# One 512-column product in place of two 256-column ones in the xbc slots, with VectorE summing the two halves

## The chip, the cores and the metric

The kernel runs on one core of one Trainium2 chip. The metric is the device time of one execution in microseconds. Three executions of the kernel before took 1444.45, 1445.17 and 1445.17 us, median 1445.17.

## The reference, cut to what matters

Two transformer blocks are computed for 256 tokens of width 1024 in fp32. The change touches the second block's mixer, and there one piece:

```
h   = rmsnorm_2(x, norm_mix_w)
u   = h @ w_in                                   # 1024 -> 3760 columns
z, xbc, dt = split(u_ssd)                        # xbc: 2048 columns
xbc = silu(causal_depthwise_conv(xbc, conv_w, conv_b))   # 4 taps along the tokens
xs, bm, cm = split(xbc)                          # feed the chunked state-space scan
```

The rest of the mixer is a 16-head latent attention (called mla here) on other columns of `u`, then the output projection.

## The kernel before, in words

Every weight matrix comes in slots of 128 x 1024 fp32. SyncE loads slot n into `ring` (three deep). ScalarE rounds it into `w_hi` (the cast, L1563), GpSimd subtracts to get the low part `w_lo` in two halves of 512 columns (L521), and TensorE multiplies. A product of fp32 quality is three products of rounded operands: high weight by high x, high weight by low x, low weight by high x. GpSimd's two halves of a slot read `ring` and `w_hi`, both in SBUF. In the expert stage VectorE does this subtraction and GpSimd does none.

The normed x stands in `h_both`, [128, 8 blocks, 512]: columns 0 to 255 of a block hold its high part, 256 to 511 its low part. The tuple `h_t` names the two halves.

The 2048 xbc columns are 16 slots, walked in the order `XBC`, each position `pos` with a PSUM bank `XBC_BANK[pos]` (2, 3, 0, 1, and then 0 and 1 in turn). `channels_slot` does one slot on TensorE: once the slot is rounded, for each of 8 blocks k the high weight block times both halves of x (L563 and L564, 256 columns each, into the same 256 columns of the bank); once the low part is there, 8 more products (L568); then it raises `spent`. A slot at `pos` of 4 or more first waits until the convolution of position `pos - 2` is done (`conv_done >= 4 * (pos - 1)`), because that one used the same bank.

On VectorE `conv(pos)` waits for `spent`, multiplies the bank's 256 columns by the row of 1/rms factors `row_x` (L2894, in place in PSUM), and applies four taps: one `tensor_scalar` (L2896) and three `scalar_tensor_tensor` (L2900), each waiting for the one before it by semaphore. ScalarE applies silu later, four positions at a time.

The order is written out by hand on each engine. On TensorE: positions 0 to 3; then 17 units of the two up-projections of the attention (`up`, L572, L573, L577), whose results VectorE and ScalarE copy out of alternate bank pairs (`up_copied`, L2912 and L2915 on VectorE; a third chunk of units may start only when the first is copied); then position 4, turns, position 5, scores of heads 0 and 1, position 6; and then the head loop, h = 0 to 15: `mla_scores(h + 2)`, `mla_turn(h)`, other turns, and `xbc(7 + h)` for h up to 8. After position 15 (h = 8) the heads 9 to 12 carry the late slots of z (`z_late`), whose second half of the first slot waits for `xdt_made >= 2`.

On VectorE: convolutions 0, 1, 2, first copy, convolution 3, more copies and rotations, convolution 4, mask and maximum of heads 0 and 1, convolution 5, and then per head h: `inverse(h + 1)`, `masked(h + 2)` (L2972, L2975), the copy of the turned probabilities (L3031), `conv(6 + h)` for h up to 9, and at some heads one of `out_lo` (L3001), `cb_mask` (L2986, L2987) or `xs_out` (L2995, L2996; the second of them raises `xdt_made` to 2 at head 8). ScalarE runs the exponentials between the masks and the inverses. Each engine takes its own list strictly in order.

Another stage holds the two forms that the change uses. The ffn's up-projection multiplies `w_hi` by a whole 512-column block of `h_both` (L1500) and the low part by 256 columns (L1503). The expert stage sums the halves of a bank with `tensor_reduce` over `"p (m t) -> p t m"` (L2792).

Of the kernel before, what the change touches and what calls it, by code (L numbers as in the profile page):

```python
# [22 lines left out]
ALU = mybir.AluOpType  # L23
# [5 lines left out]
AX = mybir.AxisListType.X  # L29

P = 128
T, D = 256, 1024
TT = T // P
KD = D // P
# [16 lines left out]
NS = 3  # L51
# [88 lines left out]
XBC_STEP = [STEP["xbc_first"] + i for i in range(4)] + [STEP["xbc"] + i for i in range(12)]  # L140
XBC_BANK = [2, 3, 0, 1] + [0, 1] * 6
# [151 lines left out]
def two_blocks(nc, weights, consts, cols_in, rows_in, x_in, mem_in, pos_in, out):  # L293
    with ExitStack() as ctx:
# [12 lines left out]
        h_both = sb("h_both", [P, KD, 2 * T], F32R)  # L307
        h_t = h_both[:, :, 0:T], h_both[:, :, T:2 * T]
        cst = sb("cst", [P, NCONST])
        cols = sb("cols", [P, NCOLS])  # L310
        rows = sb("rows", [P, NROWS])
# [13 lines left out]
        bank = ctx.enter_context(nc.psum_tensor("bank", [P, 8, 512], F32))  # L325

        def area(name, pattern=None, **kw):
            a, b = AREA[name]
            v = arena[:, a:b]
            return v.rearrange(pattern, **kw) if pattern else v  # L330
# [123 lines left out]
        def wait_slot(pe, n):  # L454

            pe.wait_ge(s["split"], n + 1)

        def wait_rounded(pe, n):

            pe.wait_ge(s["hi_made"], n + 1)  # L460
# [90 lines left out]
        def _(pe):  # L551
# [27 lines left out]
            def channels_slot(n, out_, src, ready=None):  # L579

                wait_rounded(pe, n)
                for k in range(KD):
                    if ready:
                        ready(k)
                    rounded_w(out_, both(w_parts, every, n % NS, slice(k * P, (k + 1) * P)), both(src, every, k, slice(0, T)),
                              start=(k == 0))
                wait_slot(pe, n)
                for k in range(KD):
                    mm = rest_w(out_, both(w_parts, every, n % NS, slice(k * P, (k + 1) * P)), both(src, every, k, slice(0, T)),
                                stop=(k == KD - 1))  # L590
                mm.then_inc(s["spent"], 1)
# [53 lines left out]
            every = slice(0, P)  # L645
            w_parts = (w_hi, w_lo)
# [117 lines left out]
            for i in range(5):  # L764
                g = row("diff_g") if i == 0 else row("ret_g")[:, (i - 1) * P:i * P]
                mm = pe.matmul(bank[:, 5, i:i + 1], g, ident[:, 0:1], start=True, stop=True)
# [163 lines left out]
            for i, (what, b, at) in enumerate(QUERY_ORDER):  # L930
                n = QUERY_SLOT[i]
# [210 lines left out]
            def xbc(pos):  # L1142

                if pos == 2:
                    pe.wait_ge(s["copied_act"], z0 + 2)
                if pos >= 4:
                    pe.wait_ge(s["conv_done"], 4 * (pos - 1))
                channels_slot(XBC_STEP[pos], bank[:, XBC_BANK[pos], 0:T], h_t)

            for pos in range(4):  # L1150
                xbc(pos)
# [1108 lines left out]
        def _(dve):  # L2260
# [626 lines left out]
            row_copied(area("row_x"), bank[:, 7, 0:T], 1)  # L2887
            by_head = lambda a: a.rearrange("p (h c) -> p h c", c=64)

            def conv(pos):  # L2890
                j = XBC[pos]
                dve.wait_ge(s["spent"], XBC_STEP[pos] + 1)
                b = bank[:, XBC_BANK[pos], :]
                v.tensor_tensor(b[:, 0:T], b[:, 0:T], area("row_x"), ALU.mult).then_inc(s["xbc_scaled"], 1)  # L2894
                dve.wait_ge(s["xbc_scaled"], pos + 1)
                v.tensor_scalar(xc[:, j, :], b[:, 0:T], col("xw", 4 * j + 3), col("xb", j), ALU.mult, ALU.add)\  # L2896
                    .then_inc(s["conv_done"], 1)
                for d in range(1, 4):
                    dve.wait_ge(s["conv_done"], 4 * pos + d)
                    v.scalar_tensor_tensor(out=xc[:, j, d:T], in0=b[:, 0:T - d], scalar=col("xw", 4 * j + 3 - d),  # L2900
                                           in1=xc[:, j, d:T], op0=ALU.mult, op1=ALU.add).then_inc(s["conv_done"], 1)
# [422 lines left out]
```

## Time and profile before

| | |
|---|---|
| runs of the kernel before | 1444.45, 1445.17, 1445.17 us |
| the profiled execution | 1444.22 us, its span 1442.4 us |
| TensorE matmuls, busy share of the span | 99%, 8796 instructions |
| VectorE | 66%, 2036 instructions |
| ScalarE | 58%, 1509 instructions |
| GpSimd | 62%, 717 instructions |
| granted TensorE clock | 0.998 of full speed |

Times in a profile row are microseconds from the start of the span unless they are called ns. PE is the matmul engine TensorE and PEld its loading of the stationary operand, DVE is VectorE, ACT ScalarE, POOL GpSimd. A matmul's own duration includes its way through the array, so matmuls in a stream overlap: the pace is read from the starts, or from the pieces of the chain. `[idle <- releaser]` behind an instruction is how long its engine sat before it and what ended that.

### The profile page before, as it was taken

What the parts mean: (1) busy time and instruction counts of PE and PEld (TensorE: products, weight loads), DVE (VectorE), ACT (ScalarE), POOL (GpSimd) and SP (SyncE); (2) the same over time, 40 slices, a digit from 0 to 9 for tenths busy, and PEclk for the clock granted to TensorE, in tenths of its full rate; (3) what the DMA queues carried; (4) which work ended last, traced back from release to release, by engine and by line L of the source; (5) the groups of instructions that cost most, each with busy time, mean ns of one, the idle gap of its engine ahead of it and who ended that gap; (6) DMA issues with size and microseconds to landing.
All of it is one profiled execution on the core that took longest, in us unless ns stands there. A gap on an engine that the chain in (4) does not pass through costs nothing.

```text
span 1442.4 us, 25571 instructions
## 1 busy us (share of the span) xinstructions
PE 1428.8 (99%) x8796; PEld 1275.7 (88%) x8796; DVE 946.3 (66%) x2036; ACT 835.1 (58%) x1509; POOL 899.0 (62%) x717
## 2 busy tenths in 40 slices
PE   8999999999999999999999999999999999999997
PEld 6788999999999999888888888888898889888886
DVE  4564399978889998655555554335677733477776
ACT  6576555456666666455445444448687765544454
POOL 6749898987777778100000006998954576699996
PEclk9999999999999999999999999999999999999999
DMA  7535567655555555555555555665633454465554
GB/s 257 161 103 180 180 196 235 195 171 161 157 165 162 162 156 163 185 200 195 197 190 191 197 195 186 192 184 185 196 129 103 164 158 138 137 193 189 191 188 131
DMA packets 137589, 253.08 MB, mean 175 GB/s; under 512 B 16464, under 2 KB 18896, under 8 KB 136848
## 3 DMA queue, kind: packets, MB, share of 16 engines
q1 hardware_dynamic: 135392, 243.79, 52.8%
q10 hardware_dynamic: 1872, 6.41, 1.3%
q0 software_dynamic: 224, 1.54, 0.3%
q8 instruction: 62, 1.02, 0.3%
q14 instruction: 39, 0.32, 0.1%
HBM read 248.54 MB, written 3.15 MB: 174 GB/s over the span
## 4 chain that ended last, share of the span: by engine, by line
PE 96%; POOL 1%; DVE 1%; issue 1%; ACT 1%; DMA 0%; SPq 0%; POOLq 0%; DVEq 0%; ACTq 0%
PE bank L554 13%; PE bank L555 13%; PE bank L556 13%; PE bank L577 6%; PE bank L572 6%; PE bank L573 6%; PE bank L568 5%; PE bank L1500 5%; PE bank L563 5%; PE bank L564 5%; PE bank L1503 3%; PE bank L1028 2%; PE bank L1001 2%; PE bank L1031 1%; POOL w_both L521 1%; PE bank L1240 1%
## 5 line engine op out<-in xcount | busy, mean ns | idle before, releaser
L521 POOL TENSOR_TENSOR w_both<-ring,w_both 128x512 fp32r<-128x512 f32 x694 | 881.5, 1300 | 527.7 <-ACT w_both L1563 519.4
L1563 ACT CAST w_both<-ring 128x1024 fp32r<-128x1024 f32 x452 | 474.3, 1050 | 368.4 <-PE bank L556 176.3
L2766 DVE TENSOR_TENSOR w_both<-ring,w_both 128x1024 fp32r<-128x1024 f32 x108 | 132.3, 1225 | 121.1 <-ACT w_both L1563 119.8
L554 PE MATMUL bank<-w_both,act_hi 128*128 128x512 f32 x512 | 199.8, 390 | 0.4 <-DVE act_lo L2771 0.4
L555 PE MATMUL bank<-w_both,act_hi 128*128 128x512 f32 x512 | 199.6, 390 | 0.0
L556 PE MATMUL bank<-w_both,act_lo 128*128 128x512 f32 x512 | 199.4, 389 | 0.0
L555 PE MATMUL bank<-h_both,w_both 128*128 128x256 f32 x648 | 183.6, 283 | 0.0
L554 PE MATMUL bank<-h_both,w_both 128*128 128x256 f32 x648 | 183.6, 283 | 0.0
L556 PE MATMUL bank<-h_both,w_both 128*128 128x256 f32 x648 | 183.6, 283 | 0.0
L563 PE MATMUL bank<-h_both,w_both 128*128 128x256 f32 x544 | 135.7, 288 | 0.0
L564 PE MATMUL bank<-h_both,w_both 128*128 128x256 f32 x544 | 133.3, 283 | 0.0
L554 PEld LDWEIGHTS bank<-h_both,w_both 128*128 128x128 f32 x648 | 124.5, 192 | 0.0
L556 PEld LDWEIGHTS bank<-h_both,w_both 128*128 128x128 f32 x648 | 124.5, 192 | 0.0
L555 PEld LDWEIGHTS bank<-h_both,w_both 128*128 128x128 f32 x648 | 124.5, 192 | 0.0
L554 PEld LDWEIGHTS bank<-w_both,act_hi 128*128 128x128 f32 x512 | 96.2, 188 | 20.6 <-DVE w_both L2766 0.7
L556 PEld LDWEIGHTS bank<-w_both,act_lo 128*128 128x128 f32 x512 | 96.2, 188 | 19.9
L555 PEld LDWEIGHTS bank<-w_both,act_hi 128*128 128x128 f32 x512 | 96.3, 188 | 19.1
L564 PEld LDWEIGHTS bank<-h_both,w_both 128*128 128x128 f32 x544 | 104.4, 192 | 0.2
L563 PEld LDWEIGHTS bank<-h_both,w_both 128*128 128x128 f32 x544 | 104.2, 192 | 0.4 <-DVE arena L2900 0.2
L2718 DVE TENSOR_TENSOR hots<-bank,chosen_t 128x1024 fp32r<-128x1024 f32 x64 | 78.3, 1224 | 11.1 <-PE bank L1001 7.1
L572 PE MATMUL bank<-w_both,h_both 128*128 128x512 f32 (+2 forms) x208 | 81.8, 395 | 0.3 <-issue 0.3
L568 PE MATMUL bank<-h_both,w_both 128*128 128x256 f32 x576 | 80.5, 283 | 0.0
(479 smaller groups left out, 2719.8 us busy)
## 6 DMA issues: line engine op xcount, KB each, us to landing
ring<-weights_in SPq DMA_DIRECT2D x910, 256.0 KB, 3.0
mem_kv<-arena ACTq DMA_DIRECT2D x2, 1024.0 KB, 7.1
arena<-mem_kv ACTq DMA_DIRECT2D x2, 1024.0 KB, 7.7
ring<-weights_in SPq DMA_DIRECT2D x8, 200.0 KB, 2.6
ring<-weights_in SPq DMA_DIRECT2D x8, 144.0 KB, 2.7
xres<-x_in SPq DMA_DIRECT2D x2, 512.0 KB, 5.1
arena<-mem_in POOLq DMA_DIRECT2D x1, 1024.0 KB, 8.5
arena<-rows_in ACTq DMA_DIRECT2D x2, 512.0 KB, 4.3
```

Source lines behind the costliest of these rows:

```text
L521: nc.gpsimd.tensor_tensor(w_lo[:, k, at], ring[:, k, at], w_hi[:, k, at].bitcast(F32), ALU.subtract).then_inc(s[done], 1)
L554: pe.matmul(out_, a[0], b[0], start=start, stop=False, **kw)
L555: pe.matmul(out_, a[0], b[1], start=False, stop=False, **kw)
L556: return pe.matmul(out_, a[1], b[0], start=False, stop=stop, **kw)
L563: pe.matmul(out_, w[0], b[0], start=start, stop=False, skip_group_check=True)
L564: return pe.matmul(out_, w[0], b[1], start=False, stop=False, skip_group_check=True)
L568: return pe.matmul(out_, w[1], b[0], start=False, stop=stop, skip_group_check=True)
L572: pe.matmul(out_, x[0], w[0], start=start, stop=False, skip_group_check=True)
L573: return pe.matmul(out_, x[1], w[0], start=False, stop=False, skip_group_check=True)
L577: return pe.matmul(out_, x[0], w[1], start=False, stop=stop, skip_group_check=True)
L1563: nc.scalar.copy(w_hi[:, k, :], ring[:, k, :]).then_inc(s["hi_made"], 1)
L2766: v.tensor_tensor(w_lo[:, k, :], ring[:, k, :], w_hi[:, k, :].bitcast(F32), ALU.subtract)\
```

## The change

In `xbc(pos)` the call of `channels_slot` is replaced. The high weight block now multiplies the whole 512-column block of `h_both` in one instruction, so that the bank's columns 0 to 255 collect high weight by high x and columns 256 to 511 high weight by low x; the low weight products go into columns 0 to 255 as before. `conv(pos)` first sums the bank's two halves into `xbc_sum`, 256 columns of `rows` in SBUF, and the multiplication by `row_x` takes `xbc_sum` in place of the bank. A wait on `xbc_scaled` stands between the two. The waits on `conv_done`, the banks and the order of the work stay.

```diff
-                channels_slot(XBC_STEP[pos], bank[:, XBC_BANK[pos], 0:T], h_t)
+                n, to = XBC_STEP[pos], bank[:, XBC_BANK[pos], :]
+                w = lambda k: both(w_parts, every, n % NS, slice(k * P, (k + 1) * P))
+                wait_rounded(pe, n)
+                for k in range(KD):
+                    pe.matmul(to, w(k)[0], h_both[:, k, :], start=(k == 0), stop=False, skip_group_check=True)
+                wait_slot(pe, n)
+                for k in range(KD):
+                    mm = rest_w(to[:, 0:T], w(k), both(h_t, every, k, slice(0, T)), stop=(k == KD - 1))
+                mm.then_inc(s["spent"], 1)
...
+            xbc_sum = rows[:, 0:T]
+
             def conv(pos):
                 j = XBC[pos]
                 dve.wait_ge(s["spent"], XBC_STEP[pos] + 1)
                 b = bank[:, XBC_BANK[pos], :]
-                v.tensor_tensor(b[:, 0:T], b[:, 0:T], area("row_x"), ALU.mult).then_inc(s["xbc_scaled"], 1)
-                dve.wait_ge(s["xbc_scaled"], pos + 1)
+                v.tensor_reduce(xbc_sum, b.rearrange("p (m t) -> p t m", m=2), AX, ALU.add).then_inc(s["xbc_scaled"], 1)
+                dve.wait_ge(s["xbc_scaled"], 2 * pos + 1)
+                v.tensor_tensor(b[:, 0:T], xbc_sum, area("row_x"), ALU.mult).then_inc(s["xbc_scaled"], 1)
+                dve.wait_ge(s["xbc_scaled"], 2 * pos + 2)
```

## Rows read from the trace of the kernel before

**Rows 1.** The page: busy us (share of the span), and the chain by engine.
```profile
PE 1428.8 (99%) x8796; PEld 1275.7 (88%) x8796; DVE 946.3 (66%) x2036; ACT 835.1 (58%) x1509; POOL 899.0 (62%) x717
...
PE 96%; POOL 1%; DVE 1%; issue 1%; ACT 1%; DMA 0%; SPq 0%; POOLq 0%; DVEq 0%; ACTq 0%
```

**Rows 2.** Busy us and instructions of each engine by stretch.
```profile
core 0: us, PE busy (x) PEld busy (x) DVE busy (x) ACT busy (x) POOL busy (x), PEclk, DMA share, GB/s
1008.70:1020.25 11.55, 11.55 (x98) 11.55 (x97) 7.50 (x16) 8.23 (x12) 10.80 (x10) 1.00 0.66 196
...
1056.40:1106.80 50.40, 50.40 (x394) 46.48 (x393) 43.07 (x113) 38.13 (x91) 23.69 (x19) 1.00 0.30 95
```

**Rows 3.** Loads of the stationary operand in order of time, two that waited for VectorE.
```profile
1056.40 0.19 PEld L563 LDWEIGHTS bank<-h_both,w_both 128*128 128x128 f32 x1 [0.16 <-DVE arena L2900]
...
1106.84 0.19 PEld L572 LDWEIGHTS bank<-w_both,h_both 128*128 128x128 f32 x1 [0.28 <-DVE arena L2996]
```

**Rows 4.** Pieces of the chain: start, us on the chain, what.
```profile
1008.74 0.12 PE bank L563
...
1010.64 0.96 PE bank L568 x8
...
1280.10 1.81 PE bank L1500 x8
1281.91 0.95 PE bank L1503 x8
```

**Rows 5.** VectorE's groups by line: count, busy us, mean ns.
```profile
L2792 DVE TENSOR_REDUCE work<-bank 128x256 f32<-128x512 f32 x19 | 13.1, 691 | 47.5 <-PE bank L1031 47.5
...
L2771 DVE TENSOR_TENSOR act_lo<-arena,act_hi 128x256 fp32r<-128x256 f32 x108 | 47.5, 441 | 0.5 <-ACT act_hi L1869 0.5
```

**Rows 6.** VectorE in order of time: convolution 0 and the next start.
```profile
1016.41 0.43 DVE L2894 TENSOR_TENSOR bank<-bank,arena 128x256 f32<-128x256 f32 x1
1016.88 0.54 DVE L2896 TENSOR_SCALAR arena<-bank,cols 128x256 f32<-128x256 f32 x1
1017.46 1.52 DVE L2900 SCALAR_TENSOR_TENSOR arena<-bank,cols,arena 128x255 f32<-128x255 f32 x3
1018.90 0.42 DVE L2894 TENSOR_TENSOR bank<-bank,arena 128x256 f32<-128x256 f32 x1
```

**Rows 7.** VectorE and GpSimd in order of time, at two VectorE instructions.
```profile
1043.63 1.31 POOL L521 TENSOR_TENSOR w_both<-ring,w_both 128x512 fp32r<-128x512 f32 x1
1044.22 1.00 DVE L2958 TENSOR_TENSOR arena<-arena 128x256 f32<-128x256 f32 x1
1044.88 1.50 POOL L521 TENSOR_TENSOR w_both<-ring,w_both 128x512 fp32r<-128x512 f32 x1
...
1060.75 1.27 POOL L521 TENSOR_TENSOR w_both<-ring,w_both 128x512 fp32r<-128x512 f32 x1 [1.83 <-ACT w_both L1563]
1061.32 0.74 DVE L3041 TENSOR_TENSOR head_one<-cst 128x16 fp32r<-128x16 f32 x1
```

**Rows 8.** All waits of VectorE, 1056.4 to 1106.8: us, times, longest.
```profile
DVE bank L2972 <- PE bank L1240: 1.8, 3, 1.0
DVE arena L2986 <- PE bank L1213: 1.5, 2, 0.9
DVE arena L2981 <- ACT work L2018: 1.4, 2, 1.0
DVE arena L3039 <- PE bank L1202: 0.8, 1, 0.8
```

**Rows 9.** GpSimd in order of time: three of its slots in the head loop.
```profile
1052.10 2.54 POOL L521 TENSOR_TENSOR w_both<-ring,w_both 128x512 fp32r<-128x512 f32 x2 [1.99 <-ACT w_both L1563]
...
1074.70 2.55 POOL L521 TENSOR_TENSOR w_both<-ring,w_both 128x512 fp32r<-128x512 f32 x2 [5.61 <-ACT w_both L1563]
...
1097.78 2.53 POOL L521 TENSOR_TENSOR w_both<-ring,w_both 128x512 fp32r<-128x512 f32 x2 [6.05 <-ACT w_both L1563]
```

**Rows 10.** VectorE in order of time: the first copy of the up-projections, and head 0's mask.
```profile
1024.39 0.75 DVE L2912 TENSOR_SCALAR arena<-bank,arena 128x512 f32<-128x512 f32 x1 [0.47 <-PE bank L577]
...
1051.65 0.43 DVE L2972 TENSOR_TENSOR bank<-bank,arena 128x256 f32<-128x256 f32 x1 [2.78 <-PE bank L1240]
```

## The prediction, made before the changed kernel was run

> **What bounds the kernel now.** I read the page first. TensorE is busy for 99% of the span and makes 96% of the chain that ended last [rows 1]. So time saved on TensorE comes out at the end, unless another engine is then late. The busy times by stretch come next [rows 2]. In the head loop, 1056.4 to 1106.8, where positions 7 to 15 run, TensorE is full, but VectorE is busy for 43.07 of 50.40 us, 85%, far above its 66% over the span. GpSimd is busy for 23.69 us, 47%; in the stretch of the first four positions it is busy for 10.80 of 11.55 us. Last, the waits of the weight loads [rows 3]: only twice around the change does TensorE wait for VectorE. At 1056.40 (position 7) it waits 0.16 us for the last tap of convolution 5. At 1106.84 (second half of the first z_late slot) it waits 0.28 us for L2996, the `xs_out` behind convolution 14. At these two places VectorE is already the late one, so work added to it ahead of them goes into the time.
>
> **TensorE's part.** Before, a slot has 16 high-weight products, a piece of 0.12 each on the chain, and 8 low ones in 0.96 us, so 0.12 each and 16 x 0.12 = 1.92 us for the high part [rows 4]. After, the high part is 8 products of 512 columns. The ffn has the same instruction with the same operands: 8 in 1.81 us [rows 4]. The gain is 1.92 - 1.81 = 0.10 us a slot (between 0.08 and 0.11, as the 1.81 and 0.96 are read), 16 x 0.10 = 1.6 us in all. The low part stays.
>
> The Trainium skill ("TensorE: Matmul & The Clock Gate", section "Back-to-back issue gap") puts an isolated warm gap at N/2.4 + 2.5 ns, so a merge would save 2.5 ns, 0.3 us in all. The rows of this case disagree: 0.12 us for 256 columns and 1.81/8 = 0.226 for 512 leave 0.014 us for each instruction saved. I go by the rows.
>
> **VectorE's part, the sum.** Each convolution gets one more `tensor_reduce` from PSUM, 512 elements to 256 with the same access pattern as L2792: 691 ns [rows 5]. It adds a wait by semaphore between two dependent instructions. Today L2894 lasts 0.43 us and the next starts 0.47 us after it [rows 6], so 0.04 of handing over. The step costs 0.69 + 0.04 = 0.73 us, for 16 convolutions 11.7 us of VectorE.
>
> **VectorE's part, the multiplication.** It now reads two operands from SBUF, `xbc_sum` and `row_x`; before, one came from PSUM. Its own length stays about 0.42 us (L2771, two SBUF operands, same size, takes 441 ns where GpSimd is idle [rows 5]). But rows 7 show what such an instruction does beside GpSimd. L2958 has two SBUF operands and 256 elements; it starts at 1044.22, while GpSimd's half slot runs from 1043.63 to 1044.94, and it lasts 1.00 us, to 1045.22: it stood until GpSimd was through. GpSimd's next half took 1.50 us in place of 1.27. L3041 with 16 elements lasts 0.74 us, to 1062.06, where GpSimd's half ends at 1062.02. L2894, with an operand in PSUM, starts at 1016.41 inside such a stretch of GpSimd and takes 0.43. So each multiplication that meets a half slot of GpSimd waits for its end, between 0 and 1.27 us, and in half the cases 0.2 us are put on GpSimd.
>
> The Trainium skill states this as a rule ("SBUF — State Buffer", section "Who interferes with whom"): a VectorE instruction with two SBUF inputs contends with a GpSimd instruction that reads SBUF, and whoever starts first holds the shared read port for its whole length. By that rule the trace agrees, with the 1.00 us above; `tensor_reduce` is named there as free of it.
>
> **What lies beside other work.** Convolutions 0 to 2 stand ahead of the first copy, which today starts at 1024.39 with 0.47 us of idle time before it [rows 10]. They add 3 x 0.73 = 2.2 us and their waits, three times at most 1.27. GpSimd is nearly full here, so a mean of 0.6 each: the copy starts 2.2 + 1.8 - 0.5 = 3.5 us later and ends, 0.75 long, at 1028.6. Three units of six 512-column products, 18 x 0.227 = 4.1 us, lie between the end of the first chunk at about 1024.3 and the chunk that needs the copy, at 1028.4, or 1028.0 with 0.4 us gained by then. So I count at most a stall of 0.6 here, none if the waits are short; up to 2.5 if all are long. I take 0. The same cover serves convolution 3, and VectorE then waits for TensorE again. Convolution 4 ends well before the scores of head 0, for which VectorE waits 2.78 us today [rows 10]. So at the scores of head 0 TensorE and VectorE both stand 0.6 us earlier (six slots).
>
> **What lies on the path.** From there to the `xs_out` that TensorE waits for, VectorE's list holds convolutions 5 to 14, ten of them. Ten sums: 10 x 0.73 = 7.3 us. VectorE's idle time on this stretch is 1.8 + 1.5 + 1.4 + 0.8 = 5.5 us [rows 8], and it takes up that much. The waits for the port: I laid the ten multiplications, moved by what had collected, on GpSimd's slots, moved with the TensorE slot that frees them. A slot takes 2.54 us of some 5.6. Three multiplications fall into one: convolution 5 (into the slot of 1052.10), 9 (1074.70) and 13 (1097.78) [rows 9], with 0.6, 0.75 and 0.8 us; the others fall beside. That is 2.2 us. By chance alone it would be 10 x 0.47 x 0.64 = 3.0; the ends are 0 and 10 x 1.27.
>
> The sum: -0.6 + 7.3 + 2.2 - 5.5 = +3.4 us when `xs_out` of head 8 is done. TensorE stands there already, since it gained on every slot; its gains on positions 6 to 15 are spent in waiting. What is late on the way: position 7 for convolution 5 (instead of 0.16 about 1.6 us), then position 11 for convolution 9, and last the z_late slot. Behind the stretched convolution on VectorE stand inverse, mask and copy of the next head; ScalarE's exponentials follow the mask, but each mask runs two heads ahead of the turn that needs it, so I count nothing for them. Convolution 15 comes after; no more convolutions follow it and VectorE comes back to waiting for scores. From there all engines run 3.4 us later, and TensorE fills the chain to the end. Weights are loaded ahead, the 0.2 us put on GpSimd now and then is covered there. SyncE's loads follow GpSimd and stay ahead too.
>
> The profiled execution took 1444.22 us with a span of 1442.4, so 1.8 outside. I forecast a span of 1445.8 and a profiled execution of 1447.6. The median shown is 0.95 above the profiled execution; against it I forecast 1445.17 + 3.4 = 1448.6 us.
>
> **The rivals.**
> - *No waiting for the port.* The multiplication costs what it did, 0.42. Against it speak L2958 and L3041 [rows 7]; for it, that a wait shows only where the two meet, and the phases may fall well. Then -0.6 + 7.3 - 5.5 = +1.2 us: 1446.4.
> - *TensorE keeps its gain*, the other side. VectorE's sums are taken up by its idle time everywhere, and the time falls by 1.6: 1443.6. It is decided at the z_late slot: VectorE may collect no more than its 5.5 us of idle time minus the 1.0 that TensorE gains on positions 6 to 15 before it. Ten sums would have to cost under 0.45 us each. For it: 34% of VectorE's span is idle. Against it: 0.69 for the same form, and the 0.28 us already waited there.
> - *The waits are long*, with GpSimd in step with VectorE, as both follow TensorE's slots, and the first copy is late too: ten times 0.9 and 1 to 2 us in the up-projections make -0.6 + 7.3 + 9 - 5.5 + 1.5 = +11.7 at most; with half of that waiting +6 to +7, 1452.
> - *The merge brings less* than in the ffn. Then the first six slots give 0 in place of 0.6, and the time is +4.0: a part of the forecast's own range.
>
> **How the numbers follow.** 0.2% of this kernel's time is 2.9 us, and what lies within it can hardly be told from no change. The forecast, +2.2 to +5, has 0.50, of it about 0.35 above 2.9. No waiting for the port has 0.24, within the bound. TensorE keeps its gain: 0.10, a third of which may come out below -2.9 or be some gain I don't see. Long waits: 0.15, all slower; 0.01 for the rest. So slower 0.50, same 0.46, faster 0.04. The range from 1445.7 to 1453.0 holds the forecast, the first rival and most of the long waits; the forecast's own range is 1447.4 to 1450.2.
>
> **What would show it.** In the profile after: 128 TensorE instructions fewer; the group of 512-column products in the xbc slots at 0.227 apart; a `tensor_reduce` x16 of 0.69 us; the multiplication x16 with a mean well above 0.42 and single ones near 1 us or more, each ending just behind a half slot of GpSimd. The weight load of position 7 should wait 1 to 2 us for a tap, and the z_late load 2 to 4 us for L2996's successor. VectorE's idle time in the head loop should fall below 2 us. I am wrong if the multiplications all stay at 0.42, if the z_late load does not wait longer, or if the span changes by more than that one stage does.

## The result, and the profile after

The changed kernel took 1449.62 us (median of 7 runs, 1448.18 to 1451.18), the kernel before in the same session 1445.13 (7 runs, 1444.12 to 1445.17). The ratio is 1.0033, 95% interval 1.0023 to 1.0043: slower by 4.5 us, where 3.4 were forecast. The profiled execution took 1450.12 us, its span 1448.3.

I compare the traces by three legs of the stage, each between two starts: from the first high-weight load of the xbc slots to the scores of head 0 (up-projections); from there to the second instruction of the second `xs_out`, which releases the late z slot (head loop); from there to the last `seg` product on VectorE, some 49 us on (last leg).

| us | first load | scores 0 | `xs_out` | last `seg` | legs | sum |
|---|---|---|---|---|---|---|
| before | 1008.47 | 1050.60 | 1106.10 | 1154.83 | 42.13, 55.50, 48.73 | 146.36 |
| after | 1009.16 | 1051.88 | 1110.41 | 1160.66 | 42.72, 58.53, 50.25 | 151.50 |

So +0.6 in the up-projections, +3.0 in the head loop, +1.5 in the last leg, 5.1 together. Another 0.7 of the 5.9 us between the spans lies ahead of the first load, where the code is the same; the first load starts between 1007.6 and 1009.4 in the profiles of all twelve kernels, so that is scatter.

The page of the changed kernel, its busy times and its chain by engine:

```profile
PE 1431.5 (99%) x8668; PEld 1269.4 (88%) x8668; DVE 960.5 (66%) x2052; ACT 835.7 (58%) x1509; POOL 900.3 (62%) x717
...
PE 92%; DVE 4%; POOL 1%; issue 1%; ACT 1%; DMA 0%; SPq 0%; POOLq 0%; DVEq 0%; ACTq 0%
```

Against [rows 1] TensorE has 128 instructions fewer and VectorE 16 more; VectorE's share of the chain went from 1% to 4%. The chain of the changed kernel at its first slots (start, us, what) shows TensorE's part as it was forecast:

```profile
1009.43 1.85 PE bank L1152 x8
1011.29 0.95 PE bank L568 x8
1012.24 1.84 PE bank L1152 x8
```

A slot now takes 1.85 + 0.95 = 2.80 us; before, from one group of low products to the next it was 2.88, so the gain is 0.08 a slot.

The head-loop leg by stretch, of the changed kernel and then of the one before (columns as in [rows 2]):

```profile
1051.88:1110.41 58.53, 56.18 (x359) 47.70 (x357) 54.61 (x133) 43.44 (x105) 27.92 (x22) 1.00 0.32 99
```

```profile
1050.60:1106.10 55.50, 55.50 (x436) 51.55 (x435) 46.91 (x122) 42.88 (x105) 25.55 (x21) 1.00 0.32 100
```

VectorE is busy for 54.61 - 46.91 = 7.70 us more and idle for 3.92 in place of 8.59 us, 4.67 less: 7.70 - 4.67 = 3.03, the whole difference of the leg. TensorE, full before, stands for 2.35 us of the leg. Where it stands is in its weight loads in order of time, changed kernel:

```profile
1058.40 1.68 PEld L1152 LDWEIGHTS bank<-h_both,w_both 128*128 128x128 f32 x8 [0.97 <-DVE arena L2912]
...
1081.55 1.69 PEld L1152 LDWEIGHTS bank<-h_both,w_both 128*128 128x128 f32 x8 [0.58 <-DVE arena L2912]
...
1111.14 0.19 PEld L572 LDWEIGHTS bank<-w_both,h_both 128*128 128x128 f32 x1 [2.48 <-DVE arena L3008]
```

Positions 7 and 11 wait for convolutions 5 and 9, and the late z slot waits 2.48 us where it waited 0.28 [rows 3]. VectorE's two instructions of the change, as groups of the stretch 1010 to 1120 of the changed kernel:

```profile
L2906 DVE TENSOR_TENSOR bank<-rows,arena 128x256 f32<-128x256 f32 x16 | 11.0, 690 | 0.6
L2904 DVE TENSOR_REDUCE rows<-bank 128x256 f32<-128x512 f32 x16 | 10.9, 681 | 1.4 <-PE bank L568 1.4
```

The sum is 681 ns, as [rows 5] had it. The multiplication has a mean of 690 against 0.42, and single ones tell why; VectorE first, then GpSimd, both in order of time:

```profile
1055.78 0.43 DVE L2906 TENSOR_TENSOR bank<-rows,arena 128x256 f32<-128x256 f32 x1
...
1078.00 1.37 DVE L2906 TENSOR_TENSOR bank<-rows,arena 128x256 f32<-128x256 f32 x1
...
1100.38 1.13 DVE L2906 TENSOR_TENSOR bank<-rows,arena 128x256 f32<-128x256 f32 x1
```

```profile
1053.37 2.54 POOL L521 TENSOR_TENSOR w_both<-ring,w_both 128x512 fp32r<-128x512 f32 x2 [1.85 <-ACT w_both L1571]
...
1076.55 2.54 POOL L521 TENSOR_TENSOR w_both<-ring,w_both 128x512 fp32r<-128x512 f32 x2 [5.61 <-ACT w_both L1571]
...
1099.92 2.71 POOL L521 TENSOR_TENSOR w_both<-ring,w_both 128x512 fp32r<-128x512 f32 x2 [6.06 <-ACT w_both L1571]
```

Convolutions 9 and 13 start their multiplication while GpSimd is at a slot and take 1.37 and 1.13; convolution 5 meets the last 0.13 us of one and takes 0.43. In the full trace every multiplication that starts inside a GpSimd half, long or short, ends 0.28 to 0.30 us behind the end of that half: convolution 9 at 1079.37, with the half over at 1079.09, and convolution 5 at 1056.21, with the half over at 1055.91.

The chain of the changed kernel ahead of the late z slot is convolution 14 and what stands behind it on VectorE:

```profile
1105.90 0.46 DVE work L3043
1106.36 0.61 DVE rows L2904
1106.99 0.45 DVE bank L2906
...
1109.89 0.60 DVE arena L3007
1110.49 0.61 DVE arena L3008
1111.15 0.50 PE bank L572
```

And then what I had not forecast at all. The stretches behind that stall (the granted clock is the third number from the end), and two TensorE groups in them:

```profile
1112.00:1113.00 1.00, 1.00 (x5) 0.76 (x4) 1.00 (x3) 0.82 (x5) 0.00 (x0) 0.64 0.42 154
1113.00:1114.00 1.00, 1.00 (x5) 0.35 (x5) 0.93 (x3) 0.10 (x2) 0.00 (x0) 0.50 0.09 16
1114.00:1115.00 1.00, 1.00 (x6) 0.62 (x8) 0.93 (x3) 0.92 (x1) 0.00 (x0) 0.50 0.00 0
1115.00:1116.00 1.00, 1.00 (x9) 0.67 (x6) 0.85 (x3) 0.58 (x3) 0.80 (x1) 0.65 0.00 0
```

```profile
1112.18 1.81 PE L577 MATMUL bank<-w_both,h_both 128*128 128x512 f32 x4
1113.92 1.55 PE L1269 MATMUL bank<-work,arena 128*64 128x256 f32 x8
```

TensorE had stood from 1109.1 to 1111.15; then its clock is at 0.50 of full, the level of 1.2 GHz, from between 1112 and 1113 to between 1115 and 1116. By the four rows it is there for (0.36 + 0.50 + 0.50 + 0.35) / 0.5 = 3.4 us. The kernel before has a clock of 1.00 here throughout, and the same two groups in it:

```profile
1107.87 1.08 PE L577 MATMUL bank<-w_both,h_both 128*128 128x512 f32 x4
1108.88 0.87 PE L1261 MATMUL bank<-work,arena 128*64 128x256 f32 x8
```

The differences, 0.73 + 0.68 = 1.41, are nearly all of the last leg's 1.52 us.

The up-projections: the first copy on VectorE and TensorE's load behind it, changed kernel.

```profile
1028.29 0.74 DVE L2924 TENSOR_SCALAR arena<-bank,arena 128x512 f32<-128x512 f32 x1
```

```profile
1029.10 0.19 PEld L572 LDWEIGHTS bank<-w_both,lat_hi 128*128 128x128 f32 x1 [0.72 <-issue]
1033.67 0.19 PEld L572 LDWEIGHTS bank<-w_both,lat_hi 128*128 128x128 f32 x1 [0.59 <-issue]
```

The copy comes at 1028.29, in place of 1024.39 [rows 10], and TensorE's load starts 0.07 us behind its end, 1029.03, after 0.72 us of standing. The trace gives "issue" as the cause; by the times it is the copy.

### The profile page after: what moved, and what is told of

It is laid out like the page before. It is cut to its first block, busy times and chain, and to the rows that moved or that the text cites. A ratio compares the mean times of both kernels' runs of the same rounds, so it can differ in the third digit from the quotient of the medians.

```text
span 1448.3 us, 25331 instructions
## 1 busy us (share of the span) xinstructions
PE 1431.5 (99%) x8668; PEld 1269.4 (88%) x8668; DVE 960.5 (66%) x2052; ACT 835.7 (58%) x1509; POOL 900.3 (62%) x717
## 4 chain that ended last, share of the span: by engine, by line
PE 92%; DVE 4%; POOL 1%; issue 1%; ACT 1%; DMA 0%; SPq 0%; POOLq 0%; DVEq 0%; ACTq 0%
PE bank L554 13%; PE bank L555 13%; PE bank L556 13%; PE bank L577 6%; PE bank L572 6%; PE bank L573 6%; PE bank L1508 5%; PE bank L568 5%; PE bank L563 4%; PE bank L564 4%; PE bank L1511 3%; PE bank L1028 2%; PE bank L1001 2%; PE bank L1031 1%; POOL w_both L521 1%
## 5 line engine op out<-in xcount | busy, mean ns | idle before, releaser
L555 PE MATMUL bank<-h_both,w_both 128*128 128x256 f32 x648 | 183.4, 283 | 0.0
L554 PE MATMUL bank<-h_both,w_both 128*128 128x256 f32 x648 | 183.3, 283 | 0.0
L556 PE MATMUL bank<-h_both,w_both 128*128 128x256 f32 x648 | 183.3, 283 | 0.0
L556 PEld LDWEIGHTS bank<-h_both,w_both 128*128 128x128 f32 x648 | 124.4, 192 | 0.0
L554 PEld LDWEIGHTS bank<-h_both,w_both 128*128 128x128 f32 x648 | 124.3, 192 | 0.0
L555 PEld LDWEIGHTS bank<-h_both,w_both 128*128 128x128 f32 x648 | 124.3, 192 | 0.0
L563 PE MATMUL bank<-h_both,w_both 128*128 128x256 f32 x416 | 103.2, 286 | 0.0
L564 PE MATMUL bank<-h_both,w_both 128*128 128x256 f32 x416 | 102.0, 283 | 0.0
L2726 DVE TENSOR_TENSOR hots<-bank,chosen_t 128x1024 fp32r<-128x1024 f32 x64 | 78.4, 1224 | 11.1 <-PE bank L1001 7.0
L568 PE MATMUL bank<-h_both,w_both 128*128 128x256 f32 x576 | 80.4, 283 | 0.0
L1508 PE MATMUL bank<-h_both,w_both 128*128 128x512 f32 x320 | 79.7, 391 | 0.3 <-issue 0.3
L564 PEld LDWEIGHTS bank<-h_both,w_both 128*128 128x128 f32 x416 | 79.8, 192 | 0.2
```

The source lines that it names most:

```text
L554: pe.matmul(out_, a[0], b[0], start=start, stop=False, **kw)
L555: pe.matmul(out_, a[0], b[1], start=False, stop=False, **kw)
L556: return pe.matmul(out_, a[1], b[0], start=False, stop=stop, **kw)
L563: pe.matmul(out_, w[0], b[0], start=start, stop=False, skip_group_check=True)
L564: return pe.matmul(out_, w[0], b[1], start=False, stop=False, skip_group_check=True)
L568: return pe.matmul(out_, w[1], b[0], start=False, stop=stop, skip_group_check=True)
```

## The experiments

My theory after the result: VectorE's sums and its waits for GpSimd make the head loop later, the stall that they leave at the late z slot costs a second time by the clock, and the first convolutions delay the up-projections a little. The rivals are named with each kernel. In the table "wait" is that of the late z load, the ratio is that of the fast executions (it differs from the quotient of the medians by up to 0.0004), and legs and waits are those of one profiled execution of each kernel; the medians of before are 1444.28 us for the first four (33 runs), 1444.44 for the next four (30) and 1444.59 for the last two (18).

| kernel | median us | ratio, 95% | legs | sum | wait |
|---|---|---|---|---|---|
| before | | | 42.13, 55.50, 48.73 | 146.36 | 0.28 |
| after | 1449.62 | 1.0033, 1.0023 to 1.0043 | 42.72, 58.53, 50.25 | 151.50 | 2.48 |
| e1_sum_unused | 1445.43 | 1.0011, 1.0002 to 1.0020 | 41.85, 57.23, 48.70 | 147.78 | 1.85 |
| e2_products_only | 1443.90 | 0.9996, 0.9986 to 1.0005 | 42.32, 55.05, 48.70 | 146.07 | 0.50 |
| e3_sum_only | 1446.75 | 1.0014, 1.0005 to 1.0023 | 42.13, 57.68, 48.70 | 148.51 | 1.69 |
| e4_port_only | 1445.95 | 1.0012, 1.0003 to 1.0021 | 42.15, 56.81, 48.75 | 147.71 | 0.87 |
| e5_first_five | 1444.85 | 1.0004, 0.9995 to 1.0013 | 41.71, 55.50, 48.75 | 145.96 | 0.28 |
| e6_filled | 1449.30 | 1.0034, 1.0023 to 1.0045 | 43.84, 58.53, 48.73 | 151.10 | 0.64 |
| e7_stall_alone | 1447.83 | 1.0020, 1.0010 to 1.0029 | 42.67, 57.67, 50.26 | 150.60 | 2.45 |
| e8_two_later | 1446.67 | 1.0019, 1.0010 to 1.0028 | 43.52, 55.95, 49.08 | 148.55 | none |
| e9_scalar_copies | 1446.68 | 1.0016, 1.0007 to 1.0025 | 43.31, 57.29, 48.73 | 149.33 | 2.02 |
| e10_last_twelve | 1448.75 | 1.0026, 1.0016 to 1.0037 | 42.25, 58.55, 50.30 | 151.10 | 2.47 |

Against before, median and legs agree within 0.9 us. The first leg scatters most: even e7, whose code there is that of before, has 42.67. The last one is steady (48.70 to 48.75 in eight kernels), and the parts of the loop leg add up below, so I read mechanisms from those two.

### The three parts, each by itself

**e1_sum_unused**: the changed kernel, but the multiplication reads columns 0 to 255 of the bank; nobody reads the sum, and the low part of x is left out.

```diff
-                v.tensor_tensor(b[:, 0:T], xbc_sum, area("row_x"), ALU.mult)...
+                v.tensor_tensor(b[:, 0:T], b[:, 0:T], area("row_x"), ALU.mult)...
```

> The changed kernel, but the multiplication by row_x reads the bank's columns 0 to 255 (PSUM) again; the sum is still made into rows and nobody reads it, so the low part of x is left out of the convolution's input. One SBUF operand in place of two, all else the same. Theory (the multiplication waits for GpSimd's half slot): L2906, whose mean was 690 ns, goes back to 0.42 us with none near 1 us; the first copy of the up-projections comes over 2 us earlier, the load at the z_late slot waits 1 to 1.5 us in place of 2.48, and the clock stays at full speed behind it. Time 0.5 to 1.5 us above the kernel before, 3 to 4 below the changed one. Rival (only the length of the 16 sums matters, the port does not): the multiplications drop but the time stays 4 to 4.5 us above before.

**e2_products_only**: TensorE's part alone; the sum is gone as well, and the low part of x is left out.

```diff
-                v.tensor_reduce(xbc_sum, b.rearrange("p (m t) -> p t m", m=2), AX, ALU.add)...
-                v.tensor_tensor(b[:, 0:T], xbc_sum, area("row_x"), ALU.mult)...
+                v.tensor_tensor(b[:, 0:T], b[:, 0:T], area("row_x"), ALU.mult)...
```

> The changed kernel without the sum: 512-column products on TensorE, VectorE multiplies the bank's columns 0 to 255 as before and leaves the low part of x out. Theory (the merge saves 0.08 to 0.10 us a slot): 1.3 to 1.6 us faster than before, minus nothing, since VectorE's list is the old one; the z_late load waits 1 us longer than the 0.28 of before, which gives back up to 1.0: so between -0.6 and -1.6. Rival (a 512-column product costs what two of 256 cost): within 0.2 us of before.

**e3_sum_only**: the kernel before with a sum of the same form (256 columns read twice) ahead of each convolution.

```diff
+                v.tensor_reduce(rows[:, 0:T], b[:, 0:T].unsqueeze(2).broadcast_to([P, T, 2]), AX, ALU.add)...
+                dve.wait_ge(s["xbc_scaled"], 2 * pos + 1)
```

> The kernel before with one more tensor_reduce of 512 reads to 256 outputs in every convolution (it reads columns 0 to 255 of the bank twice and writes rows, which nobody reads), old 256-column products, old multiplication. Theory (VectorE's list binds at position 7 and at z_late): ten sums of 0.73 less VectorE's 5.5 us of idle time, +1.5 to +2.5 us above before; the z_late load waits about 2 us. Rival (VectorE has 34% of idle time and hides 11.7 us of sums): no change, the z_late load waits 0.3 to 0.5 us.

**e4_port_only**: the kernel before, with the multiplication reading two operands from SBUF; the products are left out of the convolution's input.

```diff
-                v.tensor_tensor(b[:, 0:T], b[:, 0:T], area("row_x"), ALU.mult)...
+                v.tensor_tensor(b[:, 0:T], rows[:, 0:T], area("row_x"), ALU.mult)...
```

> The kernel before with one edit: the multiplication reads columns 0 to 255 of rows (SBUF) in place of the bank, so the convolution's input is left out. No sum, old products. Theory (two SBUF operands wait for GpSimd's half slot): the multiplication's mean rises from 0.42 to 0.6 or 0.7 us, single ones to over 1 us, each ending 0.3 to 0.4 us behind the end of a half slot of GpSimd; the waits are mostly taken up by VectorE's idle time, so the time rises by 0 to +1 us only. Rival (the longer multiplications in the changed kernel come from the wait on the sum just ahead, not from the port): here all 16 stay at 0.42 us.

The head-loop legs fit together to some hundredths of a us. The products alone: 55.05 - 55.50 = -0.45. The sum: 57.23 - 55.05 = +2.18 on top of the products, and 57.68 - 55.50 = +2.18 by itself. The multiplication from SBUF: 58.53 - 57.23 = +1.30 in the changed kernel, 56.81 - 55.50 = +1.31 by itself. Together -0.45 + 2.18 + 1.30 = +3.03. Each of these numbers comes from one profile of a kernel. So of the 3.48 us that VectorE's parts cost in the loop, 2.18 are the sum's and 1.30 the multiplication's. In e1 all sixteen multiplications take 431 to 433 ns; in e4 they spread (0.42 to 1.27 us). Its group, two single ones, and its weight load at the late z slot:

```profile
L2894 DVE TENSOR_TENSOR bank<-rows,arena 128x256 f32<-128x256 f32 x16 | 11.7, 729 | 1.1 <-PE bank L568 1.1
```

```profile
1054.37 1.13 DVE L2894 TENSOR_TENSOR bank<-rows,arena 128x256 f32<-128x256 f32 x1
...
1103.99 1.02 DVE L2894 TENSOR_TENSOR bank<-rows,arena 128x256 f32<-128x256 f32 x1
```

```profile
1108.72 0.19 PEld L572 LDWEIGHTS bank<-w_both,h_both 128*128 128x128 f32 x1 [0.87 <-DVE arena L2996]
```

By the Trainium skill ("SBUF — State Buffer", "Who interferes with whom") a VectorE instruction with two SBUF inputs contends with a GpSimd instruction that reads SBUF, and one with at most one SBUF input, outside the 2-port modes, does not. The pair e1 and e4 agrees, 0.43 always against a mean of 0.73. I had put e4 at 0 to +1 us, on the ground that VectorE's idle time would take it up; it cost 1.3 in the loop and 1.7 in the median. The two rows shown are convolution 5, 0.7 us longer straight ahead of position 7, where TensorE waits 0.87 in place of 0.16, and convolution 14, 0.6 longer straight ahead of the late z slot; behind neither is there idle time before TensorE needs the result.

Of the other expectations here, e3's held (+2.5 us, a wait of 1.69). In e1 the time held (+1.2), but the late z load waits 1.85 and not 1 to 1.5. e2's failed: I had put it at -0.6 to -1.6 us, and it came out at -0.4 in the median and -0.3 in the legs. Its slots do start 2.79 us apart, so its rival, that a 512-column product costs what two of 256 do, is out as well; but the gain of the first six slots does not show in its up-projection leg (42.32 against 42.13), which has single waits of 0.52 and 0.42 us where before has none above 0.05.

In none of these four does the clock fall, and in none is the last leg above 48.75. e1 stands close below the changed kernel at the late z slot:

```profile
1107.44 0.19 PEld L572 LDWEIGHTS bank<-w_both,h_both 128*128 128x128 f32 x1 [1.85 <-DVE arena L3008]
```

With 0.6 us less standing than the changed kernel it lost nothing behind it. Of the changed kernel's loss of 5.1 us, 3.0 are in the loop, 0.6 in the up-projections, and the 1.5 of the last leg are in none of its parts.

### The clock

**e7_stall_alone**: the kernel before with three sums, each waiting for the one before it, ahead of the second `xs_out`. Nobody reads them.

```diff
+                if i == 1:
+                    for r in range(3):
+                        link(v.tensor_reduce(rows[:, r * T:(r + 1) * T], bank[:, at, :].rearrange("p (m t) -> p t m", m=2), AX, ALU.add))
```

> The kernel before with one artificial delay: three tensor_reduces of 0.69 us on dead columns of rows, one after the other, ahead of the xs_out for which the z_late slot waits (2.2 us). Nothing else changed. Theory: TensorE waits 0.28 + 2.2 = 2.5 us there, and the granted clock falls behind it as in the changed kernel: +2.2 for the stall and up to +1.5 for the clock, +2.2 to +3.7. If the clock does not fall, +2.2. Rival (later stages take the delay up): under +1.

**e6_filled**: the changed kernel, TensorE repeating the products of the first half of the late z slot ahead of the wait.

```diff
-                    for k in (2 * i, 2 * i + 1):
-                        rounded_x(bank[:, 7 - 4 * t, :], x(k, t), w(k), start=(k == 0))
+                    for _ in range(3 if i == 0 and t == 0 else 1):
+                        for k in (2 * i, 2 * i + 1):
+                            rounded_x(bank[:, 7 - 4 * t, :], x(k, t), w(k), start=(k == 0))
```

> The changed kernel with TensorE busy in the stall at the z_late slot: the first half's eight products are done three times over (each round starts the sum anew, the output is the same), 1.8 us of work in place of waiting; 0.7 us of the 2.48 stay idle. VectorE's list is untouched. Theory (behind the 2.5 us stall the granted clock is 0.5 for 3 us and that costs 1.5 us more): the clock stays at 1.00 through 1112 to 1116, the shift from the stall to the weigh stage falls from 5.8 to about 4.3, and the median is 1 to 1.5 us under the changed kernel's +4.5, so +3 to +3.5. Rival (the lower clock is chance and unrelated to the stall): same as the changed kernel, +4.5, or more.

The late z load of e7, and the stretches behind it:

```profile
1110.26 0.19 PEld L572 LDWEIGHTS bank<-w_both,h_both 128*128 128x128 f32 x1 [2.45 <-DVE arena L2999]
```

```profile
1110.00:1112.00 2.00, 1.74 (x6) 1.39 (x7) 1.97 (x7) 1.50 (x5) 0.00 (x0) 0.86 0.59 193
1112.00:1114.00 2.00, 2.00 (x9) 0.95 (x9) 1.86 (x5) 1.05 (x3) 0.00 (x0) 0.50 0.05 14
1114.00:1116.00 2.00, 2.00 (x15) 1.52 (x12) 0.67 (x3) 1.28 (x4) 1.71 (x2) 0.79 0.00 0
```

A stall of 2.17 us more than before costs 2.17 in the loop leg and 1.53 in the last one, with no other part of the change in the kernel. In e6 VectorE is as late as in the changed kernel (the same 58.53), but TensorE is kept at work, and the load stands 0.64. That load and the stretches behind it:

```profile
1112.29 0.19 PEld L572 LDWEIGHTS bank<-w_both,h_both 128*128 128x128 f32 x1 [0.64 <-DVE arena L3009]
```

```profile
1112.00:1114.00 2.00, 1.78 (x8) 1.42 (x8) 1.97 (x7) 1.48 (x5) 0.00 (x0) 1.00 0.55 187
1114.00:1116.00 2.00, 2.00 (x15) 1.26 (x14) 1.86 (x5) 1.56 (x4) 0.38 (x1) 1.00 0.00 1
```

The clock stays at 1.00 and the last leg is 48.73, 1.52 less. So the drop follows TensorE's standing and not VectorE's lateness. Over all kernels: waits of 2.48, 2.45 and 2.47 us at this place (after, e7, e10) have the drop and a last leg of 50.25 to 50.30; waits of 1.85 and 2.02 (e1, e9) and all shorter ones have no drop and a last leg of 49.08 or less. At another place a longer wait went without one: in e6's own up-projections the load behind the first copy waits 2.32 us, and the clock stays at 1.00.

```profile
1030.72 0.19 PEld L572 LDWEIGHTS bank<-w_both,lat_hi 128*128 128x128 f32 x1 [2.32 <-issue]
```

The median of e6 did not show the gain: I had expected +3 to +3.5, and it is +4.9, no less than the changed kernel's. In its profile the up-projection leg is 43.84, 1.1 longer than in the changed kernel, with that stall of 2.3 us at the first copy. Whether the same holds in its other executions no profile shows.

The drop need not be in every execution. A granted clock of 0.997 over the whole execution stands in the results of the kernels that had the drop in their profiles (3 of 7 executions of the changed kernel, 4 of 11 of e7, 2 of 8 of e10) and in e6's two slowest of 8, and in no other execution whose clock is on record. The eleven of e7 fall into two groups: 1445.77 to 1446.44 us (four, at 0.998 or 0.999) and 1447.69 to 1449.16 (seven, among them all four at 0.997). That fits a stall which is followed by the drop in some executions and not in others, and a second drop, elsewhere, in some of e6; but the profiles show one execution each, so this is not shown.

### The up-projections

**e5_first_five**: the merge at positions 0 to 4 alone; the low half is copied to SBUF and added in the bank, so that no instruction has two SBUF operands.

```diff
+                if pos > 4:
+                    return channels_slot(XBC_STEP[pos], bank[:, XBC_BANK[pos], 0:T], h_t)
...
+                if pos <= 4:
+                    v.tensor_copy(xbc_sum, b[:, T:2 * T])...
+                    v.tensor_tensor(b[:, 0:T], b[:, 0:T], xbc_sum, ALU.add)...
+                v.tensor_tensor(b[:, 0:T], b[:, 0:T], area("row_x"), ALU.mult)...
```

> The merge only for positions 0 to 4, where VectorE has idle time behind it, and a sum with one SBUF operand: VectorE copies the bank's columns 256 to 511 to rows, adds them to columns 0 to 255 in the bank, and multiplies as before (0.42 + 0.42 + two hand-overs, 0.9 us more per convolution). Positions 5 to 15 as before. The output is complete. Theory (TensorE's gain stays where VectorE has cover): five slots, -0.4 to -0.5 us in the stretch, the first copy of the up-projections is at 1027.2 and just not late; in the median -0.5 to 0. Rival (a sum costs wherever it stands, or the first copy is late here too): +0.5 or more.

**e10_last_twelve**: the change at positions 4 to 15 alone.

```diff
+                if pos < 4:
+                    return channels_slot(XBC_STEP[pos], bank[:, XBC_BANK[pos], 0:T], h_t)
...
+                if pos >= 4:
+                    v.tensor_reduce(xbc_sum, b.rearrange("p (m t) -> p t m", m=2), AX, ALU.add)...
+                v.tensor_tensor(b[:, 0:T], xbc_sum if pos >= 4 else b[:, 0:T], area("row_x"), ALU.mult)...
```

> Positions 0 to 3 (those beside the up-projections) are as in the kernel before, positions 4 to 15 as in the changed kernel. Theory (the first convolutions' waits for GpSimd delay the first up-projection copies): the leg from the first product to the scores is back at about 42.1 us, the head loop's leg stays at 58.0 to 58.6, the clock falls behind the stall as in the changed kernel and the last leg is 50.25; total +3.5 to +4.3 us against the kernel before, 0.4 to 1.5 below the changed kernel. Rival (the first four convolutions cost nothing, the leg's differences are scatter between executions): the leg is 42.7 or more and the total stays at about +4.5. A third way: with an earlier start the stall at the last masked rows is just as long or shorter, and if it is below 2 us the clock stays up and the total is +2.5 to +3.

e10 has its first copy on VectorE early again:

```profile
1026.07 0.74 DVE L2928 TENSOR_SCALAR arena<-bank,arena 128x512 f32<-128x512 f32 x1
```

No load waits in its up-projections for longer than 0.41, the leg is back at 42.25, and the other two stay as in the changed kernel (58.55, 50.30). The theory's numbers held (+4.2 in the median), the third way did not come: with an earlier start the stall is just as long. The leg alone would not tell this from scatter, since e7 has 42.67 with the code of before; the stall at the copy does. In the profiles of the kernels that have the whole change at the first four positions it is 0.7 (after), 2.3 (e6) and 1.5 (e8), in e9 it is 1.6, and in all others 0.31 or less. So this term is between 0.7 and 2.3 us in three profiles, though the code here is the same.

Two things make it. One is what the convolutions take: from the start of convolution 0 to the first copy it is 7.4 us with the old ones (e2, e7, e10), 9.6 with the sums (e1, e3) and 11.1 with sums and port waits (after, e6, e8). The other is when VectorE starts into convolution 0: 7.98 us behind TensorE's first load in the changed kernel, 8.7 in e8 and 9.6 in e6, and their stalls grow by the same steps (0.72, 1.45, 2.32). e5 and e9 show it too. They have the same instructions here, and from the start of convolution 0 to the first copy both take 10.2 us; but convolution 0 starts 8.1 us behind TensorE's first load in e5, which has no stall, and 9.8 in e9. Ahead of it VectorE works on `lat_lo`, for which it waits on ScalarE in both; these two rows are e5's and e9's.

```profile
1013.98 2.05 DVE L2308 SCALAR_TENSOR_TENSOR lat_lo<-bank,cols,lat_hi 128x256 fp32r<-128x256 f32 x5 [3.69 <-ACT lat_hi L1598]
```

```profile
1015.05 2.05 DVE L2323 SCALAR_TENSOR_TENSOR lat_lo<-bank,cols,lat_hi 128x256 fp32r<-128x256 f32 x5 [2.94 <-ACT lat_hi L1602]
```

e5's -0.4 us in the legs is five slots' gain. Its median is at +0.4, where I had expected -0.5 to 0, and the interval of its ratio holds 1, so the median can't tell a gain from nothing; its profile is of its fastest execution.

### Two ways around the loss

**e8_two_later**: the changed kernel with convolutions 14 and 15 moved behind the copies of heads 9 and 10, past the second `xs_out`.

```diff
-                if 6 + h < 16:
+                if h < 8:
...
+                elif h in (9, 10):
+                    conv(5 + h)
```

> The changed kernel with convolutions 14 and 15 moved on VectorE behind the copies of heads 9 and 10 (from 8 and 9), so that the xs_out for which z_late waits comes one convolution earlier. The output is complete. Theory (what is late is VectorE's list at z_late): the load there waits under 0.5 us, the clock stays full, about 3.2 us less on TensorE at that place; the stalls ahead of it stay (up-projections 1.2 us, positions 7 and 11). Median 0 to +2 above before. Rival (the delay only moves to mla_out of heads 8 and 9 or to the state-space part behind): +3 or more.

There is no wait for VectorE at the late z slot and no drop of the clock; the loop leg is 55.95 and the last one 49.08. The stall at the first copy (1.5 us) is in its total, +2.2. I had expected 0 to +2, so that is just missed. With the loop at +0.5 in place of +3.0 this gives back more of the loop than e9, and it needs no cheaper instruction, only another order.

**e9_scalar_copies**: the merge everywhere, but ScalarE copies the low half to SBUF (VectorE for positions 0 to 3) and VectorE adds it in the bank.

```diff
+            def low_out(pos):
+                act.wait_ge(s["spent"], XBC_STEP[pos] + 1)
+                ...
+                nc.scalar.copy(low_copy(pos), bank[:, XBC_BANK[pos], T:2 * T]).then_inc(s["x_loaded"], 1)
...
-                v.tensor_reduce(xbc_sum, b.rearrange("p (m t) -> p t m", m=2), AX, ALU.add)...
-                v.tensor_tensor(b[:, 0:T], xbc_sum, area("row_x"), ALU.mult)...
+                v.tensor_tensor(b[:, 0:T], b[:, 0:T], low_half, ALU.add)...
+                v.tensor_tensor(b[:, 0:T], b[:, 0:T], area("row_x"), ALU.mult)...
```

> All sixteen positions keep the merged products, and the reduction goes: the bank's low half is copied to SBUF (by ScalarE at positions 4 to 15, by VectorE at positions 0 to 3), and VectorE adds it to the high half in the bank, with one operand in SBUF, so that nothing of the convolution waits for GpSimd. The output is complete. Theory (the loss is made of additions on VectorE beyond its idle time, of waits for GpSimd, and of the clock that falls behind the 2.5-us stall): ten additions of about 0.47 us are 4.7 us, below the 5.5 us of idle time, so the leg from the scores to the last masked rows is 55.0 to 56.0 us (before 55.50, changed kernel 58.53), TensorE waits under 1 us at the load of the last masked rows, the clock stays at 1.00 and the last leg is 48.7; total -1.0 to +0.5 us against the kernel before. Rival (ScalarE can't carry 0.46 us more per head): its casts and exponentials come late, positions 8 to 15 wait for ScalarE, leg 57 us or more, total +1 us or more.

The theory's number failed: the leg is 57.29, not 55 to 56, and the total +2.1; both are what the rival had (57 or more, +1 or more). The additions take 428 ns, the multiplications 432, no port wait is left, and yet the late z load waits 2.02. VectorE still had 3.4 us of waits in the leg that it could not use, and one of them is of the change's own making. VectorE and ScalarE of e9 in order of time:

```profile
1098.76 0.43 DVE L2930 TENSOR_TENSOR bank<-bank,rows 128x256 f32<-128x256 f32 x1 [0.72 <-ACT rows L2054]
```

```profile
1096.11 1.34 ACT L1988 ACTIVATE arena<-arena 128x256 f32<-128x256 f32 x4
1097.36 1.03 ACT L1577 CAST w_both<-ring 128x1024 fp32r<-128x1024 f32 x1
1098.30 0.36 ACT L2054 COPY rows<-bank 128x256 f32<-128x256 f32 x1
```

ScalarE's copy stood behind four silus and a cast, so the rival's reason, ScalarE, accounts for 0.7 of the 3.4 us; the rest (1.7 us of waits for scores, 0.8 for other work of TensorE, 0.3 for exponentials) is idle time that lies where TensorE was late in its turn. "Idle time minus added time" is too kind a sum: it holds where each wait lies behind the added work and ahead of the next point that TensorE needs.

No version of the merge that beats the kernel before came out of this. With the work in this order even e2, without any work on VectorE for it, gives only -0.3 us in the legs, ratio 0.9996 with an interval that holds 1. The merge at five positions (e5) is at -0.4 in the legs.

## Why the prediction was right, and where it was not

- **Direction and size.** Forecast 1448.6, range 1445.7 to 1453.0; measured 1449.62. The forecast's difference was +3.4, the measured one +4.5 (+3.3 to +6.2 by the interval of the ratio).
- **TensorE's gain.** Forecast 0.10 a slot (its own terms, 1.92 - 1.81, give 0.11), measured 0.08, in the stated bounds. The rule of the Trainium skill that I had weighed ("TensorE: Matmul & The Clock Gate", "Back-to-back issue gap"), 2.5 ns for each instruction saved, would by estimate give 0.02 a slot; the trace disagrees with it again. That the gain of the later slots is spent in waiting held: e2 has 10 slots' gain, 0.8 us, in its loop leg and keeps 0.45 of it, while the late z wait grows from 0.28 to 0.50.
- **The sums.** Forecast 0.69 + 0.04 each. Measured 0.68, and 0.72 from the start of the sum to that of the multiplication (0.70 to 0.73).
- **The waits for the port.** Forecast 2.2 us over convolutions 5 to 14, at 5, 9 and 13. Measured 1.8: 0.94 at 9, 0.70 at 13, 0.12 at 10 and none at 5. Convolution 5 came at 1055.78, with the slot over at 1055.91, where I had it 0.6 ahead of the end. The price of one was read a little wrong as well: L2958 ends at 1045.22, 0.28 behind GpSimd's half [rows 7], and not with it.
- **The idle time.** Forecast that VectorE uses up 5.5 us. It used 4.67 over the leg and has 0.6 left behind the first mask. The loop: forecast +4.0, measured +3.0. The added work was near the forecast: from start to start the ten sums took 7.1 us and the multiplications 1.9 more than before, 9.0 against 9.5. Some 1.1 us of that did not count, which is in no term of the forecast: where VectorE no longer waits, its next instruction starts up to 0.1 us ahead of the end of the one before, as the one at 1018.90 does in [rows 6].
- **The places.** Position 7 waits 0.97 (forecast about 1.6), position 11 waits 0.58, the late z load 2.48 (forecast 2 to 4).
- **The up-projections.** Forecast a gain of 0.6 with a stall counted as 0, at most 2.5. Measured a loss of 0.6, with stalls of 0.72 and 0.59; the multiplications of convolutions 1 to 3 took 1.15 to 1.22 us. I had the copy at 1028.6 in its end and TensorE needing it at 1028.0 to 1028.4, and rounded that to nothing; it ended at 1029.03, and TensorE was ready at 1029.10 - 0.72 = 1028.38. This term was mis-sized by 1.2 us, and other profiles show it larger.
- **The step that failed**: "From there all engines run 3.4 us later, and TensorE fills the chain to the end." In the profiled execution they ran 5.1 later (3.4 - 1.0 + 1.2 + 1.5), and TensorE did not fill the chain as before: behind a stall of 2.48 us its clock was at half for 3.4 us, 1.5 us that are in no term of the sum. That the median came out within 1.1 us of the forecast is in part luck: two errors of opposite sign stand against each other, the loop (1.0 too much) and the up-projections and the clock (2.7 too little).
- **The rivals.** "No waiting for the port" is out: e4 has the waits alone. "TensorE keeps its gain" would have needed sums under 0.45; e9, with additions of 0.46 from start to start, lies at that mark and lost 1.8 us in the loop. "The waits are long" was right on the late first copy and wrong on the loop.

## What to carry to other kernels

Merging two TensorE instructions saved about 0.01 us each here (0.08 for eight); any work that it puts on another engine must be cheaper than that where that engine is the late one, and VectorE, busy for 85% of the loop, was late at two points of it. When a forecast leaves TensorE standing for some us at one place, look for the clock behind it and price it from a row at the lower level: here a stall of 2.5 us cost 4. And an operand moved from PSUM to SBUF is not free beside a busy GpSimd: 1.3 us in the loop here, for ten instructions whose own length did not change.

## What the runs showed of the hardware that I had not expected

- The clock fell to 0.50 for 3.4 us behind a single stall of 2.45 to 2.48 us at the late z slot, in a TensorE that is busy for 99% of its span, in the profiles of all three kernels with such a stall, and cost 1.52 to 1.57 us each time; behind 1.85 and 2.02 us there, and behind 2.32 us at the first copy of e6, it did not fall.
- A multiplication that waits for GpSimd ends 0.28 to 0.30 us behind GpSimd's half. The one at 1100.38 ends at 1101.51, with the half over at 1101.22, and L2958 ended 0.28 behind its half as well [rows 7]. L3041, with 16 elements in place of 256, ended 0.04 behind. Convolution 5, whose multiplication starts 0.13 us ahead of the end of a half, loses nothing.
- Costs of one engine's added work were additive to 0.01 us in the single profiles where the points at which TensorE waits stayed the same (2.18 and 2.18, 1.30 and 1.31), though the single waits fell on other convolutions in e4 (5, 6, 10, 11 and 14) than in the changed kernel (9, 10 and 13).
